# The order of the three products of a split weight piece on TensorE

## The chip, the cores and the metric

The kernel runs on one core of one Trainium2 chip. The metric is the device time of one launch, in microseconds (us): the median of the runs shown, lower is better. The profile is of one execution on the same kind of chip.

## The reference, cut to what matters

Two transformer blocks run one after the other on a sequence of 256 rows of width 2048, in float32. What matters here are the dense products: activations times weight matrices.

```python
proj = h @ w_in                                  # first block, 9,296 columns
return x + gate[:, None, :] * (concat([ya, yb]) @ w_out)
z = h @ w_in + b_in                              # second block, 8,200 columns
m = sigmoid(g_attn) * (attn @ w_attn_o) + sigmoid(g_pool) * (pool @ w_pool_o)
return m @ w_out
return (gelu(gate) * val) @ w_down               # gate, val from h @ w_up, convolved over 3 rows
```

Between them stand RMS norms, two attentions in the first block, one attention and a windowed mean in the second. The second block has 16 rows more (its meta rows), of which most products need 258 or 272 columns.

## The kernel before, in words

**Split products.** Every float32 factor is split into a rounded half (`hi`, type float32r) and the remainder (`lo`, also float32r). A product is then the sum of three matmuls: `w_lo`·`a_hi`, `w_hi`·`a_lo` and `w_hi`·`a_hi`. All add up in the same PSUM bank.

**Pieces and panels.** A weight matrix comes in pieces of 128 x 1024 floats: two blocks of 128 input rows (`kp` = 2) by 512 output columns. A panel is 512 output columns; it takes J = 8 pieces (4 where only 1024 input rows are there). Its four groups of 128 output columns go to four PSUM banks. The weights are the stationary operand and the activations (256, 258 or 272 columns) stream past. So a piece is 4 banks x 2 blocks x 3 products = 24 matmuls, and a bank collects products over all pieces of its panel. The class `Job` lists the panels in their order: qidx0, strip, qidx1, qk_a (4 panels), v_a (2), qk_b (4), v_b (2), z_a (2), z_b (2), out_a (4), out_b (4), qkv2 (6), f2, u2 (2), g2 (8), attn_o (3), pool_w, attn_o3, pool_o (4), out2 (4), up (22), down (11). The panels strip and f2 write one bank only, bank 3. The job pool_w and the job down have matmul code of their own (L1042 and after, L1100 and after), the rest go through `panel` of `pe_program` (L731).

**The path of a piece.** There are four slots for raw, `hi` and `lo` each. SyncE issues the DMA into `raw[s]` once `lo_ready[s]` tells that the old content was used. ScalarE (`split`, L1170) copies it rounded into `w_hi[s]` and raises `hi_ready[s]`; before that it waits for `used[s]`, which TensorE raises with the last matmul of the piece that had the slot. VectorE (`split`, L1660) waits for `hi_ready[s]`, subtracts, writes `w_lo[s]` and raises `lo_ready[s]`. TensorE waits for `lo_ready[s]` at the head of the piece.

**The banks.** In the last piece of a panel the last matmul of bank b raises `acc_ready[b]`. ScalarE or VectorE then takes the bank out of PSUM and raises `acc_free[b]`. In the first piece of the next panel TensorE waits for `acc_free[b]` ahead of its first matmul into bank b. All panels use the same four banks `acc`, but for `up`, where the panels alternate between `acc` and `val` (the other four, named psum_x and psum_y in the profile).

**Who takes the banks out.** This is written by hand as steps behind a certain piece of the next panel, in the queue of that engine, one bank after the other:
- ScalarE, behind the split of piece 2: `stored` (L1273) for qidx, v and z panels; with a second instruction per bank (`squares`, L1277) for qk_a and qk_b, and the bank is freed by this second one; `biased` (L1415) for qkv2, u2, g2; `mixed_stored` (L1539 and L1542) for out2, where ScalarE then also waits for its own second instruction before it goes on to the next bank; `conv_first` (L1593) for up.
- VectorE, behind the split of piece 1: `residual` for out_a and out_b, `times_gate` for attn_o and pool_o (both are recorded at L1654, the line of the helper `stt`).

In the panels of a hardware loop (`Fori`) the instructions that take out a bank have addresses that the engine computes in registers, behind its wait. At the end of out_b and of out2 the squares of the new values are summed (L955, L958), and the next panel can't begin before the norm that follows from them.

**Work between pieces.** TensorE does small matmuls and transposes of the attention behind certain pieces (`after`), in program order. Where `acts` is given, TensorE also waits at each piece for the activations' `lo` half, which VectorE makes behind its split of a piece.

Of the kernel before, what the change touches and what calls it, by code (L numbers as in the profile page):

```python
# [28 lines left out]
P = 128  # L29
# [78 lines left out]
def at_least(eng, sem, value):  # L108

    if isinstance(value, int) and value <= 0:  # L110
        return
    eng.wait_ge(sem, value)
# [10 lines left out]
def ada_sums(M, g):  # L123

    return (M.ada_first, M.ada_acc)[g // 2][:, (g % 2) * PIECE:(g % 2 + 1) * PIECE]


class Chain:
# [5 lines left out]
    def step(self, ins, wait=True):  # L134
        ins.then_inc(self.sem, 1)
        self.n += 1
        if wait:
            self.wait()
# [586 lines left out]
def pe_program(M, pe):  # L725

    job = M.job
# [3 lines left out]
    def panel(job, i, after={}, acts=None, pair=None, value=None):  # L731

        acc, ready, free = (M.acc, M.acc_ready, M.acc_free) if value is None else (M.val, M.val_ready, M.val_free)
        stored = [n + (i if pair is None else pair) for n in job.free0] if value is None else [value] * 4
        for j in range(job.J):
            s = j % SLOTS
            pe.wait_ge(M.lo_ready[s], job.raw0 + job.turn(i, j) + 1)
            if acts is not None:  # L740
                pe.wait_ge(M.act_ready, acts + job.kp * (j + 1))
            for b in job.banks:
                col = 0 if len(job.banks) == 1 else b * P
                out = acc[b][:, 0:job.N]
                if j == 0:
                    at_least(pe, free[b], stored[b])
                for k in range(job.kp):
                    c = job.kp * j + k
                    last = c == job.kp * job.J - 1
                    a_hi, a_lo = job.rhs(c)  # L750
                    w_hi = M.hi[s][:, k * job.cols + col:k * job.cols + col + P]
                    w_lo = M.lo[s][:, k * job.cols + col:k * job.cols + col + P]
                    pe.matmul(out, w_lo, a_hi, start=c == 0, stop=False)  # L753
                    pe.matmul(out, w_hi, a_lo, start=False, stop=False)  # L754
                    ins = pe.matmul(out, w_hi, a_hi, start=False, stop=last)  # L755
                if j == job.J - 1:
                    ins.then_inc(ready[b], 1)
            if j < job.J - 1:
                ins.then_inc(M.used[s], 1)
            for step in after.get(j, ()):  # L760
                step()

    def transpose(out, src, rows=P):
        return pe.transpose(out, src, ident[0:rows, 0:rows])
# [10 lines left out]
    for k in range(DC):  # L775
        out = M.acc[k % 4]
# [3 lines left out]
        for t in range(2):  # L780
            ins = transpose(out[:, META + t * P:META + (t + 1) * P], M.x_rows[:, t * D + k * P:t * D + (k + 1) * P])
# [13 lines left out]
    for g in range(4):  # L795
        pe.wait_ge(M.lo_ready[3], 4 * (g + 1))
        for m in range(8):
            ins = pe.matmul(M.X[:, 8 * g + m:8 * g + m + 1], ada_sums(M, g)[:, m * P:(m + 1) * P],
                            ones[:, 0:1], start=True, stop=True)
        ins.then_inc(M.ada_cols, 1)  # L800


    panel(job["qidx0"], 0, acts=M.mk["qidx0"])
    panel(job["strip"], 0)

    def k_idx_sums():
# [7 lines left out]
    def k_idx_twice():  # L814
# [3 lines left out]
                  ).then_inc(M.kd_ready, 1)  # L818

    panel(job["qidx1"], 0, {0: [k_idx_sums], 5: [k_idx_twice]})  # L820


# [90 lines left out]
    b = job["qk_b"]  # L913
# [128 lines left out]
    for j in range(4):  # L1042
        pe.wait_ge(M.lo_ready[j], w.raw0 + 1)
        pe.wait_ge(M.act_ready, M.mk["pool_w"] + 2 * (j + 1))
        for e in range(2):
            b_ = (2 * j + e) % 4
            pe.wait_ge(M.acc_free[b_], w.free0[b_] + j // 2)
            for k in range(2):
                a_hi, a_lo = w.rhs(2 * j + k)
                w_hi = M.hi[j][:, k * 256 + e * P:k * 256 + (e + 1) * P]  # L1050
                w_lo = M.lo[j][:, k * 256 + e * P:k * 256 + (e + 1) * P]
                out = M.acc[b_][:, 0:LIVE]
                pe.matmul(out, w_lo, a_hi, start=k == 0, stop=False)
                pe.matmul(out, w_hi, a_lo, start=False, stop=False)
                ins = pe.matmul(out, w_hi, a_hi, start=False, stop=k == 1)
# [14 lines left out]
    for k in range(DC):  # L1070
        pe.wait_ge(M.sq_done, 33 + k)
        ins = pe.matmul(M.X[:, 512:512 + LIVE], ones[:, 0:P], M.sqr[:, (k % 4) * ROWS:(k % 4) * ROWS + LIVE],
                        start=k == 0, stop=k == DC - 1)
# [1093 lines left out]
```

## Time and profile before

| what | value |
|---|---|
| median of 3 runs | 2143.71 us (2142.81 to 2145.34) |
| profiled execution: span, first to last instruction | 2141.7 us |
| median less span | 2.0 us |
| TensorE matmul busy | 2010.6 us, 94% of the span |
| VectorE busy | 1282.3 us, 60% |
| ScalarE busy | 991.1 us, 46% |
| mean granted TensorE clock | 0.968 of full |

The page gives no time of its own for the profiled execution beside its span; the median of the runs stands 2.0 us over the span. Matmuls overlap in the pipeline, so the sum of their durations is over the busy time; what counts for the rate is the distance from start to start.

### The profile page before, as it was taken

The numbers are of one execution on the slowest core, as the hardware profiler recorded it, in microseconds if no ns is written. First come the engines' busy times: TensorE is split into PE (matmuls) and PEld (weight loads), VectorE is DVE, ScalarE is ACT, GpSimd is POOL, SyncE is SP. The second block draws the span as 40 slices with busy tenths as digits, with TensorE's granted clock in tenths as the row PEclk, the third lists the DMA queues.
The fourth block names the chain that finished last, engine by engine and source line by source line (L and its number), as shares of the span: only waits on it lengthen the run. The fifth ranks groups of instructions, "written<-read, shape, count | busy, mean of one in ns | idle before, by whom it ended". The sixth has DMA issues, their size and how long they took to land.

```text
span 2141.7 us, 39022 instructions
## 1 busy us (share of the span) xinstructions
PE 2010.6 (94%) x15084; PEld 1911.8 (89%) x15084; DVE 1282.3 (60%) x1565; ACT 991.1 (46%) x1429; POOL 143.8 (7%) x151
## 2 busy tenths in 40 slices
PE   4169999999999999999999999799999999999997
PEld 2169999999999899988899999699999999988886
DVE  6777885685567633444447664666556666664555
ACT  3034555554554444444344444454444444444443
POOL 0000000000002000000004111100000000000000
PEclk8579999999999999999999999899999999999999
DMA  8868665475555555644444555255655665665553
GB/s 308 307 192 286 224 196 175 137 251 182 158 168 188 156 171 157 185 145 138 146 137 142 189 189 179 78 177 174 189 178 175 185 186 177 189 204 189 193 190 124
DMA packets 179903, 391.62 MB, mean 183 GB/s; under 512 B 11955, under 2 KB 17632, under 8 KB 177376
## 3 DMA queue, kind: packets, MB, share of 16 engines
q1 hardware_dynamic: 178800, 388.03, 57.0%
q10 hardware_dynamic: 1024, 2.51, 0.3%
q8 instruction: 54, 0.88, 0.2%
q14 instruction: 25, 0.20, 0.0%
HBM read 388.39 MB, written 2.10 MB: 182 GB/s over the span
## 4 chain that ended last, share of the span: by engine, by line
PE 89%; DVE 4%; DMA 4%; ACT 2%; issue 1%; DVEq 0%; SPq 0%; POOLq 0%; POOL 0%; ACTq 0%
PE acc L753 20%; PE acc L755 20%; PE acc L754 20%; DMA raw<-in_w_ada 4%; PE psum_y L754 2%; PE psum_y L755 2%; PE psum_x L754 2%; PE psum_x L755 2%; PE psum_y L753 2%; PE psum_x L753 2%; PE acc L1123 2%; PE acc L1122 2%; PE acc L1121 2%; PE psum_y L1123 1%; PE psum_x L1123 1%
## 5 line engine op out<-in xcount | busy, mean ns | idle before, releaser
L1660 DVE TENSOR_TENSOR w_lo<-raw,w_hi 128x1024 fp32r<-128x1024 f32 (+1 forms) x644 | 814.0, 1271 | 727.2 <-ACT w_hi L1170 723.9
L1170 ACT ACTIVATE w_hi<-raw 128x1024 fp32r<-128x1024 f32 (+1 forms) x644 | 675.2, 1050 | 929.1 <-PE acc L755 602.4
L753 PE MATMUL acc<-act_hi,w_lo 128*128 128x258 f32 (+2 forms) x3424 | 983.5, 287 | 16.9 <-issue 9.3
L755 PE MATMUL acc<-act_hi,w_hi 128*128 128x258 f32 (+2 forms) x3424 | 974.9, 285 | 0.0
L754 PE MATMUL acc<-act_lo,w_hi 128*128 128x258 f32 (+2 forms) x3424 | 972.8, 284 | 0.0
L753 PEld LDWEIGHTS acc<-act_hi,w_lo 128*128 128x128 f32 x3424 | 651.9, 190 | 27.7 <-issue 26.2
L754 PEld LDWEIGHTS acc<-act_lo,w_hi 128*128 128x128 f32 x3424 | 650.4, 190 | 0.7 <-issue 0.5
L755 PEld LDWEIGHTS acc<-act_hi,w_hi 128*128 128x128 f32 x3424 | 650.7, 190 | 0.0
L754 PE MATMUL psum_y<-act_lo,w_hi 128*128 128x258 f32 x352 | 100.1, 284 | 0.0
L755 PE MATMUL psum_y<-act_hi,w_hi 128*128 128x258 f32 x352 | 100.0, 284 | 0.0
L754 PE MATMUL psum_x<-act_lo,w_hi 128*128 128x258 f32 x352 | 99.8, 284 | 0.0
L755 PE MATMUL psum_x<-act_hi,w_hi 128*128 128x258 f32 x352 | 99.8, 283 | 0.0
L753 PE MATMUL psum_y<-act_hi,w_lo 128*128 128x258 f32 x352 | 99.4, 282 | 0.0
L753 PE MATMUL psum_x<-act_hi,w_lo 128*128 128x258 f32 x352 | 99.3, 282 | 0.0
L1123 PE MATMUL acc<-w_hi,down_hi 128*128 128x512 f32 x176 | 69.3, 394 | 0.0
L1122 PE MATMUL acc<-w_lo,down_hi 128*128 128x512 f32 x176 | 69.0, 392 | 0.0
L1121 PE MATMUL acc<-w_hi,down_lo 128*128 128x512 f32 x176 | 68.3, 388 | 0.0
L716 POOL TENSOR_TENSOR ffn_act<-gelu_gate,conv_val 128x1024 f32 x11 | 34.5, 3135 | 503.5 <-DVE conv_val L1654 503.5
L753 PEld LDWEIGHTS psum_y<-act_hi,w_lo 128*128 128x128 f32 x352 | 67.2, 191 | 0.0
L755 PEld LDWEIGHTS psum_y<-act_hi,w_hi 128*128 128x128 f32 x352 | 66.9, 190 | 0.0
L754 PEld LDWEIGHTS psum_y<-act_lo,w_hi 128*128 128x128 f32 x352 | 66.8, 190 | 0.0
L755 PEld LDWEIGHTS psum_x<-act_hi,w_hi 128*128 128x128 f32 x352 | 66.8, 190 | 0.0
(291 smaller groups left out, 2186.6 us busy)
## 6 DMA issues: line engine op xcount, KB each, us to landing
raw<-in_w_in SPq DMA_DIRECT2D x272, 512.0 KB, 3.6
raw<-in_w_ffn_up SPq DMA_DIRECT2D x176, 512.0 KB, 3.9
raw<-in_w_ffn_down SPq DMA_DIRECT2D x88, 512.0 KB, 3.5
raw<-in_w_ada SPq DMA_DIRECT2D x64, 512.0 KB, 5.2
raw<-in_w_out SPq DMA_DIRECT2D x64, 512.0 KB, 4.1
ada_x<-in_w_ada SPq DMA_DIRECT2D x16, 1024.0 KB, 7.3
raw<-in_w_attn_o SPq DMA_DIRECT2D x16, 512.0 KB, 3.6
raw<-in_w_pool_o SPq DMA_DIRECT2D x16, 512.0 KB, 4.4
```

Source lines behind the costliest of these rows:

```text
L716: pool.tensor_tensor(M.F[:, ds(i * 4 * SEQ, 4 * SEQ)], M.gg[:, :], M.vt[:, :], ALU.mult).then_inc(M.F_ready, 1)
L753: pe.matmul(out, w_lo, a_hi, start=c == 0, stop=False)
L754: pe.matmul(out, w_hi, a_lo, start=False, stop=False)
L755: ins = pe.matmul(out, w_hi, a_hi, start=False, stop=last)
L1121: pe.matmul(out, d_lo, w_hi, start=start, stop=False)
L1122: pe.matmul(out, d_hi, w_lo, start=False, stop=False)
L1123: ins = pe.matmul(out, d_hi, w_hi, start=False, stop=stop)
L1170: act.activation(M.hi[s][:, 0:job.width], M.raw[s][:, 0:job.width], ACT.Copy).then_inc(M.hi_ready[s], 1)
L1660: dve.tensor_tensor(M.lo[s][:, 0:job.width], M.raw[s][:, 0:job.width], M.hi[s][:, 0:job.width].bitcast(FP32), ALU.subtract).then_inc(M.lo_ ...
```

## The change

TensorE waits at the head of a piece for the rounded half only. For all banks and blocks it runs `w_hi`·`a_lo` and `w_hi`·`a_hi` (16 matmuls). Then it waits for the remainder half and runs `w_lo`·`a_hi` for all banks and blocks (8 matmuls). The signals `acc_ready[b]` and `used[s]` are raised by the last matmul as before, which is now one of the last eight. No other engine's code is changed.

```diff
         for j in range(job.J):
             s = j % SLOTS
-            pe.wait_ge(M.lo_ready[s], job.raw0 + job.turn(i, j) + 1)
+            pe.wait_ge(M.hi_ready[s], job.hi0 + job.turn(i, j) + 1)
             if acts is not None:
                 pe.wait_ge(M.act_ready, acts + job.kp * (j + 1))
             for b in job.banks:
@@
                 for k in range(job.kp):
                     c = job.kp * j + k
-                    last = c == job.kp * job.J - 1
                     a_hi, a_lo = job.rhs(c)
                     w_hi = M.hi[s][:, k * job.cols + col:k * job.cols + col + P]
+                    pe.matmul(out, w_hi, a_lo, start=c == 0, stop=False)
+                    pe.matmul(out, w_hi, a_hi, start=False, stop=False)
+            pe.wait_ge(M.lo_ready[s], job.raw0 + job.turn(i, j) + 1)
+            for b in job.banks:
+                col = 0 if len(job.banks) == 1 else b * P
+                for k in range(job.kp):
+                    c = job.kp * j + k
+                    a_hi, a_lo = job.rhs(c)
                     w_lo = M.lo[s][:, k * job.cols + col:k * job.cols + col + P]
-                    pe.matmul(out, w_lo, a_hi, start=c == 0, stop=False)
-                    pe.matmul(out, w_hi, a_lo, start=False, stop=False)
-                    ins = pe.matmul(out, w_hi, a_hi, start=False, stop=last)
+                    ins = pe.matmul(acc[b][:, 0:job.N], w_lo, a_hi, start=False, stop=c == job.kp * job.J - 1)
                 if j == job.J - 1:
                     ins.then_inc(ready[b], 1)
             if j < job.J - 1:
```

## Rows read from the trace of the kernel before

**Rows 1.** The page: busy us, share of the span, instructions of each engine.
```profile
PE 2010.6 (94%) x15084; PEld 1911.8 (89%) x15084; DVE 1282.3 (60%) x1565; ACT 991.1 (46%) x1429; POOL 143.8 (7%) x151
```

**Rows 2.** The page: the chain that ended last, by engine.
```profile
PE 89%; DVE 4%; DMA 4%; ACT 2%; issue 1%; DVEq 0%; SPq 0%; POOLq 0%; POOL 0%; ACTq 0%
```

**Rows 3.** The page, groups: busy us, mean ns | idle us before, releaser.
```profile
L753 PE MATMUL acc<-act_hi,w_lo 128*128 128x258 f32 (+2 forms) x3424 | 983.5, 287 | 16.9 <-issue 9.3
```

**Rows 4.** Waits of TensorE: waiter <- releaser: total us, times, longest.
```profile
PE acc L753 <- DVE act_lo L1654: 5.7, 5, 3.8
PE acc L753 <- ACT store L1273: 1.2, 2, 0.6
```

**Rows 5.** Timeline of VectorE in qidx0: start us, us, instruction [idle <-releaser].
```profile
139.19 1.23 DVE L1660 TENSOR_TENSOR w_lo<-raw,w_hi 128x1024 fp32r<-128x1024 f32 x1 [0.46 <-ACT w_hi L1170]
141.39 0.88 DVE L1654 SCALAR_TENSOR_TENSOR act_lo<-squares,shift,act_hi 128x256 fp32r<-128x256 f32 x2 [0.18 <-ACT act_hi L1199]
```

**Rows 6.** Windows: length, PE, PEld, DVE, ACT, POOL busy (instructions), clock, DMA share, GB/s.
```profile
612.00:655.00 43.00, 43.00 (x382) 43.00 (x380) 29.67 (x45) 21.58 (x28) 0.33 (x1) 1.00 0.53 173
655.00:701.00 46.00, 46.00 (x392) 46.00 (x391) 30.52 (x33) 21.82 (x28) 14.11 (x12) 1.00 0.64 199
735.00:855.00 120.00, 120.00 (x955) 120.00 (x955) 47.43 (x40) 51.15 (x59) 0.00 (x0) 1.00 0.58 171
1250.00:1343.00 93.00, 93.00 (x771) 93.00 (x771) 43.92 (x42) 46.23 (x69) 12.70 (x16) 1.00 0.56 184
708.70:712.70 4.00, 4.00 (x18) 4.00 (x19) 3.24 (x8) 1.69 (x4) 0.00 (x0) 0.50 0.00 0
```

**Rows 7.** Timeline, end of the first v_a panel.
```profile
315.90 0.28 PE L755 MATMUL acc<-act_hi,w_hi 128*128 128x256 f32 x1
316.22 0.39 ACT L1273 ACTIVATE store<-acc 128x256 f32<-128x256 f32 x1 [0.34 <-PE acc L755]
```

**Rows 8.** Timeline, end of the second g2 panel, in a loop.
```profile
971.33 0.28 PE L755 MATMUL acc<-act_hi,w_hi 128*128 128x258 f32 x1
971.78 0.48 ACT L1415 ACTIVATE gates<-acc,bias_gates 128x258 f32 x1 [0.25 <-PE acc L755]
```

**Rows 9.** Timeline, from the last qkv2 panel to f2.
```profile
855.62 0.29 PE L755 MATMUL acc<-act_hi,w_hi 128*128 128x272 f32 x1
855.94 0.58 ACT L1415 ACTIVATE qkv<-acc,bias_qkv,scale_qkv 128x272 f32<-128x272 f32 x1 [0.18 <-PE acc L755]
856.67 0.36 PE L753 MATMUL acc<-act_hi,w_lo 128*128 128x272 f32 x1 [0.76 <-ACT qkv L1415]
```

**Rows 10.** Groups by shape: instructions that take out banks; busy us, mean ns.
```profile
L1654 DVE SCALAR_TENSOR_TENSOR gates<-gates,acc 128x258 f32<-128x258 f32 x24 | 10.1, 423 | 10.5 <-PE acc L755 10.4
L1654 DVE SCALAR_TENSOR_TENSOR rT<-acc,gate,rT 128x256 f32<-128x256 f32 x20 | 9.3, 481 | 4.0 <-PE acc L755 4.0
```

**Rows 11.** Timeline of ScalarE at the end of a qk_a panel.
```profile
236.78 0.37 ACT L1273 ACTIVATE store<-acc 128x256 f32 x1
237.04 0.38 ACT L1277 ACTIVATE squares<-acc 128x256 f32<-128x256 f32 x1
237.31 0.39 ACT L1273 ACTIVATE store<-acc 128x256 f32 x1
```

**Rows 12.** Timeline of ScalarE at the end of the first out2 panel.
```profile
1272.54 0.48 ACT L1539 ACTIVATE gates<-acc,cols 128x258 f32 x1 [0.24 <-ACT squares L1542]
1272.91 0.38 ACT L1542 ACTIVATE squares<-acc 128x258 f32<-128x258 f32 x1
1273.53 0.48 ACT L1539 ACTIVATE gates<-acc,cols 128x258 f32 x1 [0.24 <-ACT squares L1542]
```

**Rows 13.** Timeline, end of the last out2 panel.
```profile
1342.80 0.29 PE L755 MATMUL acc<-act_hi,w_hi 128*128 128x258 f32 x1
1342.94 0.48 ACT L1539 ACTIVATE gates<-acc,cols 128x258 f32<-128x258 f32 x1
1343.81 0.48 ACT L1539 ACTIVATE gates<-acc,cols 128x258 f32<-128x258 f32 x1
```

## The prediction

> **What bounds the kernel now.** I read the page's busy shares first, then the chain, the groups, the waits of TensorE, and last the timeline around each place where one panel follows another. TensorE is busy 94% of the span [rows 1] and makes up 89% of the chain that ended last [rows 2]; no other engine has more than 4%. The reader is to see in the groups how little is left to win: before the first product of a bank and block (L753, the one that the old order puts behind the wait for the remainder) TensorE was idle 16.9 us in all its 3424 executions on `acc` [rows 3]. In the waits the idle time that is put down to an engine's work ends with `act_lo` (5.7 us, 5 times) or with ScalarE taking out a bank (1.2 us, 2 times) [rows 4]; the rest, 9.3 us put to issue [rows 3], stands behind the norms ahead of qkv2 and up. None ends with `w_lo`. So the weights' remainder is nowhere late, and the program is a stream of matmuls whose length is count times distance. That distance is m = 0.1126 us in out_a (382 in 43.00 us), 0.1173 in out_b, 0.1257 in qkv2 (272 columns), 0.1206 in out2 (258 columns) [rows 6].
>
> **Part 1, the earlier start: 0 us.** The head of a piece waits for `w_hi` instead of `w_lo`, some 1.2 us sooner [rows 5]. In the stream both have been there for long. Where TensorE does wait with weights at stake, in qidx0, it waits for `act_lo`, and VectorE writes that behind the `w_lo` of the same piece: `w_lo` starts at 139.19, the two `act_lo` end at 142.27 [rows 5]. The new order still needs `act_lo` in its first matmul, so nothing starts sooner. Bounds: a loss is excluded, since `w_hi` is always there before `w_lo`; a gain is at most the 5.7 us of rows 4. I take 0. The second wait, now in the middle of a piece, is met; what queues behind it is the rest of TensorE's own stream, and everyone waits for that. Nothing is issued anew: the same 24 matmuls and weight loads per piece, no DMA moved, and `used[s]` is raised at the same place of the stream, so ScalarE's splits and SyncE's transfers keep their times.
>
> **Part 2, the distance of the matmuls: 0 us.** The same pairs come as before (each load of `w_hi` twice, `w_lo` once; `a_hi` streams twice, `a_lo` once). Only the neighbours change, and a bank changes every 4 and every 2 matmuls instead of every 6. The trace doesn't show that order. The nearest rows are those of out_a and out_b, 4.7 ns apart for the same 256 columns [rows 6]; they differ in where the activations lie, which the change leaves alone, so I take a tenth of it, 0.5 ns, to either side: 13,152 matmuls in `panel` (548 piece-equivalents of 24) times 0.5 ns = 6.6 us either way.
>
> **Part 3, the banks are ready later: +18 us.** This is what the change costs. The last matmul of bank b in a panel used to stand 6(3-b) matmuls ahead of the panel's last one, now 2(3-b). Bank 0 was ready 18 matmuls before the end, 2.1 us; now 6, 0.7 us. And the next panel reaches bank b after 4b matmuls, not 6b. Call the start of the last matmul 0. Then:
> - The engine starts taking out a bank d after the start of its last matmul: 316.22 - 315.90 = 0.32 us [rows 7]; in a hardware loop 971.78 - 971.33 = 0.45 us, because the addresses are computed behind the wait [rows 8].
> - TensorE starts r after the bank was taken out: 856.67 - (855.94 + 0.58) = 0.15 us [rows 9]. For VectorE I take the same r and d.
> - Bank 0 is free for TensorE at -6m + d + e + r, with e the time it takes; TensorE would come at m. Stall: d + e + r - 7m. Banks 1 to 3 add (p - 4m) each where the period p from bank to bank is over 4m, about 0.48.
>
> By kind of boundary (e from rows; where waits are met, instructions of ScalarE follow each other 0.1 us before the end of the last, as 0.37 us ones every 0.27 [rows 11]):
> - qk_a, qk_b, 8 boundaries, copy and squares: e = 0.27 + 0.38 = 0.65, p = 0.53 [rows 11], m = 0.118 (out_b's, rounded up). Loop: 0.45 + 0.65 + 0.15 - 0.83 = 0.42, and 3 x 0.06 = 0.18: 0.6 us, 6 times; outside a loop 0.47, twice. Together 4.5 us.
> - out2, 3 boundaries in a loop: e = 0.37 + 0.38 = 0.75 and p = 1273.53 - 1272.54 = 0.99, because ScalarE waits for its own result [rows 12]. 0.45 + 0.75 + 0.15 - 0.84 = 0.51, and 3 x (0.99 - 0.48) = 1.53: 2.04 us, together 6.1 us.
> - The end of out2, whose sums TensorE and the norm wait for: the period is 0.87 there, the last copy starts at 1343.81 [rows 13]. New: bank 0 is ready at 1342.80 - 0.72 + 0.32 = 1342.40, the last copy starts 3 x 0.87 later, at 1345.01: +1.2 us on the path. At the end of out_b VectorE is still at a split when bank 0 gets ready, nothing changes.
> - qkv2, 5 in a loop: e = 0.58 [rows 9]: 0.45 + 0.58 + 0.15 - 0.88 = 0.30, together 1.5 us. From qkv2 to f2, which needs bank 3 at once: four in a row with p = 0.47 from -0.43 on end at 1.56, TensorE starts at 1.71 instead of 856.67 - 855.62 = 1.05 [rows 9]: 0.65 us. The same from qidx0 to strip with short copies: 0.1.
> - g2: e = 0.48 [rows 8]. Loop 0.24, 6 times; outside 0.11, twice: 1.7 us.
> - out_a and out_b on VectorE: e = 0.48 [rows 10]. 0.32 + 0.48 + 0.15 - 0.79 = 0.16, 4 times; in out_b's loop 0.45 + 0.48 + 0.15 - 0.82 = 0.26, 3 times: 1.4 us.
> - attn_o and pool_o: e = 0.42 [rows 10]: 0.05, 6 times, and 0.18 in a loop, twice: 0.7 us.
> - u2 0.08 twice; 8 boundaries with one copy of 0.39 us [rows 7]: 0.02 each; up to down, where VectorE's two steps per bank follow: 0.3. Together 0.6 us.
> - up, 22 panels: 0. They alternate between two sets of banks, a set has a whole panel of time.
>
> Sum: 4.5 + 6.1 + 1.2 + 1.5 + 0.65 + 0.1 + 1.7 + 1.4 + 0.7 + 0.6 = 18.4 us. What hid the taking out of the banks before were the 2.1 us of other banks' matmuls; with 0.7 us the cover is gone. A stall of TensorE adds in full, as nothing else limits the stream behind it. Bounds of this part: 12 us, if only the squares, out2 and half of the rest come as worked out; 24 us, if in loops the waits keep ScalarE from overlapping (p = e + 0.05: 0.14 x 3 x 5 = 2 us more in qkv2, 0.05 x 3 x 6 = 1 us in g2, 0.2 x 6 in qk) and d is 0.1 longer than read at a dozen places.
>
> Against span: 2141.7 + 18.4 = 2160.1; the median of the runs lies 2.0 us above the span, which gives 2162.1 us, 0.86% slower.
>
> What the rows show on cover (bank 0 taken out beside 18 matmuls into other banks) is also a rule of the Trainium skill, Perfetto Trace Analysis, Optimizing Tensor Performance, Matmuls: "Independent matmul groups should rotate through different PSUM banks so the ACT/DVE evacuation of one overlaps the next group's matmuls". By it this change goes the wrong way, since it closes all four groups nearly together; the size it leaves to the trace. The same page, Matmul Optimizations, wants all 8 banks used, which here only `up` does, where I count no loss.
>
> **The rivals.**
> 1. *The matmuls come closer together, and the kernel is faster.* The place is the distance within the stream. For it: the same 256 columns are seen at 112.6 and 117.3 ns [rows 6], so something beside the columns counts, and it may be which weights load beside which stream. Against: every pair of load and stream of the new order exists in the old one. It decides from 18.4 us / 13,152 = 1.4 ns on; at 3 ns it gives 2162 - 39 = 2123 us. 4%.
> 2. *The earlier start counts.* If TensorE's waits in qidx0 were in truth for the weights, 5.7 us return and the boundaries still cost: 2156 us. Against it speaks rows 4. 4%.
> 3. *The banks are taken out in time.* If r and d are shorter where TensorE isn't idle yet, short copies cost nothing and only out2 is left, its end included: 7 us, 2151 us; with out2's period pressed too, 2145 us. For it: d is read against modelled ends of matmuls. Against: the wait from qkv2 to f2 shows d and r end to end. 10%, of which 3 points within 0.2% of before.
> 4. *Stalls pull the clock down.* Behind the idle time ahead of qkv2, one of the two that make up the 9.3 us of rows 3, the granted clock is 0.50, the 1.2 GHz level, and 4 us hold 18 matmuls (0.222 us each, not 0.126) [rows 6]. Some 20 matmuls at that level cost 2 us; at the 11 boundaries of qk and out2 that is 22 us: 2184 us. Against: behind 0.76 us of idle at f2 [rows 9] the next matmuls are at full rate, and my stalls are 0.5 us pieces. 6%.
>
> **How the numbers follow.** Forecast 76%, with 2151 to 2173 as its own range (12 to 24 us, and the 6.6 us of the distance taken partly). I predict 2162 us. The range 2150 to 2174 leaves out rival 1, rival 4 and the lowest part of rival 3. A measurement tells about 0.2% (4.3 us) from no change. Faster: 4%, from rival 1. Same: 5%, from rival 3 and a weak form of 1. Slower: 91%.
>
> **What would show it.** Right: at the head of out2 panels TensorE idles about 0.5 us four times, ended by ScalarE's L1542; at qk panels by L1277; at qkv2 and g2 by L1415, once each; none in up. The waits of TensorE for ScalarE and VectorE at banks grow from some 2 us (1.2 in rows 4, 0.76 in rows 9) to some 19 us; the count of matmuls per us within the windows away from boundaries stays within 0.5%. Wrong: if the window counts change by over 1%, part 2 fails; if boundaries of qkv2 and g2 show no idle time, d or r fails; if idle time ends with `w_lo`, part 1 fails.

## The result, and the profile after

The changed kernel takes 2161.65 us (median of 4 runs, 2160.96 to 2163.53) against 2143.26 us (4 runs, 2141.08 to 2145.34): a ratio of 1.0087 with a 95% interval of 1.0073 to 1.0101. It is 18.4 us slower; 2162 us had been forecast. The profiled execution has a span of 2159.4 us, 1.9 us under its time, and a granted clock of 0.97 as before.

The page of the changed kernel: busy us, share and instructions of each engine; the chain by engine; the three products in `panel`, which are now L751, L752 and L760 (busy us, mean ns | idle us before, releaser).

```profile
PE 2023.0 (94%) x15084; PEld 1914.0 (89%) x15084; DVE 1277.7 (59%) x1565; ACT 977.7 (45%) x1429; POOL 150.5 (7%) x151
PE 88%; DVE 4%; DMA 4%; ACT 2%; issue 2%; ACTq 0%; DVEq 0%; SPq 0%; POOLq 0%; POOL 0%
L751 PE MATMUL acc<-act_lo,w_hi 128*128 128x258 f32 (+2 forms) x3424 | 865.4, 289 | 23.5 <-issue 9.3
L752 PE MATMUL acc<-act_hi,w_hi 128*128 128x258 f32 (+2 forms) x3424 | 849.8, 284 | 0.0
L760 PE MATMUL acc<-act_hi,w_lo 128*128 128x258 f32 (+2 forms) x3424 | 485.9, 284 | 0.0
```

The counts of instructions on these engines are the same [rows 1]. Only the first product of a bank waits, as before, and its idle time went from 16.9 [rows 3] to 23.5 us. The product with the remainder, L760, waits for nothing: its own wait in the middle of a piece costs nothing. The busy time of TensorE rose by 12.4 us with the same matmuls. That isn't work, for the matmuls are the same: a matmul that is held at the head of a bank is recorded longer, and its neighbours cover part of the stall, as the timeline below shows.

The waits of TensorE in the changed kernel (waiter <- releaser: total us, times, longest):

```profile
PE acc L751 <- issue: 9.3, 2, 4.7
PE acc L751 <- DVE act_lo L1659: 6.1, 6, 3.8
PE acc L751 <- ACT squares L1547: 3.2, 12, 0.3
PE acc L751 <- ACT qkv L1420: 1.4, 1, 1.4
PE acc L751 <- ACT store L1278: 1.3, 2, 0.7
PE acc L751 <- ACT squares L1282: 1.0, 6, 0.2
```

New against [rows 4] are 12 waits for the second instruction of out2 and 6 for that of the qk panels; the one wait for `qkv` is that of f2, 0.76 us before [rows 9]; the 5.7 us for `act_lo` are still there, 6.1 now, and `w_lo` is still in no row.

The timeline of TensorE in the changed kernel at the first boundary between two out2 panels, and its waits at the next two of that panel's banks (start us, us, instruction [idle <-releaser]):

```profile
1309.09 0.76 PE L760 MATMUL acc<-act_hi,w_lo 128*128 128x258 f32 x5
1310.17 0.39 PE L751 MATMUL acc<-act_lo,w_hi 128*128 128x258 f32 x1 [0.31 <-ACT squares L1547]
1310.39 0.28 PE L752 MATMUL acc<-act_hi,w_hi 128*128 128x258 f32 x1
...
1311.16 0.39 PE L751 MATMUL acc<-act_lo,w_hi 128*128 128x258 f32 x1 [0.25 <-ACT squares L1547]
1312.16 0.39 PE L751 MATMUL acc<-act_lo,w_hi 128*128 128x258 f32 x1 [0.25 <-ACT squares L1547]
```

ScalarE there:

```profile
1309.37 0.48 ACT L1544 ACTIVATE gates<-acc,cols 128x258 f32 x1 [1.26 <-PE acc L760]
1309.74 0.38 ACT L1547 ACTIVATE squares<-acc 128x258 f32<-128x258 f32 x1
1310.36 0.48 ACT L1544 ACTIVATE gates<-acc,cols 128x258 f32 x1 [0.24 <-ACT squares L1547]
```

The last of the five remainders ends at 1309.85, so it began at 1309.57. From there to 1310.17 are 0.60 us where 0.12 is the distance: a stall of 0.48 us, of which the idle column shows 0.31. ScalarE takes a bank every 0.99 us, and TensorE then follows at 1311.16 and 1312.16, at that same period. The matmul behind a stalled one comes 0.22 us later instead of 0.12.

The place of the cost is seen best by cutting the trace at the first matmul of each stage. Us from one to the next in the profiled execution: the kernel before, and what each kernel has on top of it. (The last four are experiments 1 to 4 below.)

```
stretch                     before   changed last_old ends_old last_new out2_later
qidx0 to qk_a                 58.70     0.14    -0.05     0.05     0.26     0.16
qk_a (4 panels)              104.58     2.13    -0.22    -0.18     1.87     2.15
v_a                           47.30     0.22    -0.16    -0.18     0.35     0.16
qk_b (4)                     114.04     2.12    -0.21    -0.13     1.65     2.13
v_b                           47.35     0.16    -0.18    -0.16     0.26     0.12
z_a to out_a                 112.05     0.09    -0.14     0.06     0.45    -1.41
out_a to qkv2 (8)             96.42     2.36    -0.02     0.01     2.98     3.18
qkv2 to f2 (6)               148.00     2.81    -0.62    -0.26     2.10     2.07
f2 to g2                      54.93     0.01    -0.23    -0.17     0.15     0.01
g2 to attn_o (8)             239.47     1.37    -0.51    -0.35     1.47     1.35
attn_o to out2 (8)            99.01     1.37    -0.22    -0.05     1.43     1.45
out2, first to last matmul    92.73     6.50     2.23     0.22     4.33     3.33
out2's last matmul to up      26.79    -0.69    -1.84     0.38    -0.69    -1.38
up, first to last matmul     516.33     0.84    -1.39     0.49    -0.76     0.61
up's last matmul to the end  255.78     0.14    -0.01    -0.02     0.16     0.13
sum                         2013.47    19.59    -3.58    -0.31    16.00    14.06
```

Together 19.6 us. The start of qidx0 lies at 128.23 before and 126.39 in the changed kernel, which makes the difference of the spans 17.8 us; that start varied from 125.28 to 128.64 among the eleven kernels profiled here.

### The profile page after: what moved, and what is told of

It is laid out like the page before. It is cut to its first block, busy times and chain, and to the rows that moved or that the text cites. A ratio compares the mean times of both kernels' runs of the same rounds, so it can differ in the third digit from the quotient of the medians.

```text
span 2159.4 us, 39115 instructions
## 1 busy us (share of the span) xinstructions
PE 2023.0 (94%) x15084; PEld 1914.0 (89%) x15084; DVE 1277.7 (59%) x1565; ACT 977.7 (45%) x1429; POOL 150.5 (7%) x151
## 3 DMA queue, kind: packets, MB, share of 16 engines
q10 hardware_dynamic: 1024, 2.51, 0.3%
## 4 chain that ended last, share of the span: by engine, by line
PE 88%; DVE 4%; DMA 4%; ACT 2%; issue 2%; ACTq 0%; DVEq 0%; SPq 0%; POOLq 0%; POOL 0%
PE acc L751 21%; PE acc L752 20%; PE acc L760 19%; DMA raw<-in_w_ada 4%; PE psum_x L760 2%; PE psum_y L751 2%; PE psum_y L752 2%; PE psum_x L752 2%; PE psum_y L760 2%; PE psum_x L751 2%; PE acc L1128 2%; PE acc L1127 2%; PE acc L1126 2%; PE psum_x L1128 1%; PE psum_y L1128 1%
## 5 line engine op out<-in xcount | busy, mean ns | idle before, releaser
L751 PE MATMUL acc<-act_lo,w_hi 128*128 128x258 f32 (+2 forms) x3424 | 865.4, 289 | 23.5 <-issue 9.3
L752 PE MATMUL acc<-act_hi,w_hi 128*128 128x258 f32 (+2 forms) x3424 | 849.8, 284 | 0.0
L751 PEld LDWEIGHTS acc<-act_lo,w_hi 128*128 128x128 f32 x3424 | 651.4, 190 | 43.1 <-issue 28.3
L752 PEld LDWEIGHTS acc<-act_hi,w_hi 128*128 128x128 f32 x3424 | 653.1, 191 | 0.7 <-issue 0.5
L760 PE MATMUL acc<-act_hi,w_lo 128*128 128x258 f32 (+2 forms) x3424 | 485.9, 284 | 0.0
L760 PEld LDWEIGHTS acc<-act_hi,w_lo 128*128 128x128 f32 x3424 | 444.1, 190 | 0.0
L752 PE MATMUL psum_y<-act_hi,w_hi 128*128 128x258 f32 x352 | 89.1, 284 | 0.0
L751 PE MATMUL psum_y<-act_lo,w_hi 128*128 128x258 f32 x352 | 89.1, 285 | 0.0
L752 PE MATMUL psum_x<-act_hi,w_hi 128*128 128x258 f32 x352 | 88.3, 283 | 0.0
L751 PE MATMUL psum_x<-act_lo,w_hi 128*128 128x258 f32 x352 | 88.2, 282 | 0.0
L752 PEld LDWEIGHTS psum_y<-act_hi,w_hi 128*128 128x128 f32 x352 | 67.4, 192 | 0.0
L751 PEld LDWEIGHTS psum_y<-act_lo,w_hi 128*128 128x128 f32 x352 | 67.2, 191 | 0.0
L751 PEld LDWEIGHTS psum_x<-act_lo,w_hi 128*128 128x128 f32 x352 | 66.9, 190 | 0.0
L752 PEld LDWEIGHTS psum_x<-act_hi,w_hi 128*128 128x128 f32 x352 | 66.9, 190 | 0.0
L760 PE MATMUL psum_x<-act_hi,w_lo 128*128 128x258 f32 x352 | 57.6, 286 | 0.0
L760 PE MATMUL psum_y<-act_hi,w_lo 128*128 128x258 f32 x352 | 56.5, 283 | 0.0
```

Of the source, the lines that this page charges most:

```text
L751: pe.matmul(out, w_hi, a_lo, start=c == 0, stop=False)
L752: pe.matmul(out, w_hi, a_hi, start=False, stop=False)
L760: ins = pe.matmul(acc[b][:, 0:job.N], w_lo, a_hi, start=False, stop=c == job.kp * job.J - 1)
```

## The experiments

The kernels of experiments 1 to 4 ran beside the same 21 runs of the kernel before (2143.18 us). The ratios are to the kernel before.

**1. `last_old`: the old order in the last piece of a panel alone.** It shows what the banks' late closing costs, and leaves the earlier start and the new order in all other pieces.

```diff
+            if j == job.J - 1:
+                ...   # wait for lo_ready at the head; per bank w_lo*a_hi, w_hi*a_lo, w_hi*a_hi
+            else:
+                ...   # the changed order
```

> The changed kernel, but in the last piece of each panel the three products of a bank stand together as before, behind the wait for the remainder; all other pieces keep the new order. Theory A (banks are ready late and are needed early): the banks of a panel are ready 18, 12, 6 and 0 matmuls before its end again, so the stall on bank 0 goes everywhere. What stays is that the first piece of the next panel comes to bank b after 4b matmuls, not 6b. By the times of the kernel before that matters in out2 alone: bank 3 is free at 2.02 + 0.15 us after the panel's start and is wanted at 1.45, some 0.7 us with the restart, and bank 2 some 0.2: 2.7 us over three boundaries. 2146 us. TensorE waits on L1282 and L1420 at no boundary of qk, qkv2 or g2. Rival B (the order within a piece costs time by itself, 1.4 ns per matmul): 7 of 8 pieces keep the new order, 2143.3 + 16 = 2159 us.

2143.16 us (11 runs; before 2143.18, 21 runs), ratio 0.9996 (0.9987 to 1.0005). B is refuted: with the banks closed early the loss is gone. A said 2146: its 2.7 us in out2 came as 2.23, but in the trace the other stretches from qidx0 on became shorter, up by 1.4 us and the rest by 0.0 to 0.6 each, together 4.0 us, and the one from out2 to up by 1.8 more (on that one see part 3 below). The trace is of the fastest of the 11 executions (2136.97 us), so its span says less than the median. The waits:

```profile
PE acc L769 <- ACT squares L1565: 0.7, 3, 0.3
PE acc L769 <- DVE act_lo L1677: 5.6, 5, 3.8
```

3 waits at banks of out2 instead of 12 and none for the qk panels; the wait for `act_lo` stays. From start to start there are two stalls per boundary, at bank 2 (0.30 us where 0.12 is the distance) and at bank 3 (0.53).

**2. `ends_old`: the old order in the first and the last piece,** the new one in between.

```diff
+            if j in (0, job.J - 1):
+                ...   # the old order, the wait for lo_ready at the head
```

> The changed kernel with the old order in the first and the last piece of each panel; the 6 (of 8) or 2 (of 4) pieces between keep the new one. Theory A: nothing is left of the cost, and the earlier start is worth nothing: 2143.3 us, within 0.1% of before. Rival B (order costs by itself): 0.7 of the pieces are new, 2143.3 + 13 = 2156 us. Rival C (the earlier start does bring something that the boundaries hid): faster than before, by up to the 5.7 us of TensorE's waits for act_lo, 2138 us.

2143.09 us (11 runs), ratio 0.9998 (0.9989 to 1.0008). A is confirmed; B (2156) and C's 2138 are refuted, and a gain of more than 2.4 us lies outside the interval. In most of the program's pieces the new order costs nothing and brings nothing that could be measured, neither by the earlier start nor by the distance (out_a to qkv2 0.01, up 0.49 over 516 us).

**3. `last_new`: the kernel before with the new order in the last piece alone.**

```diff
+            if j < job.J - 1:
+                ...   # the old order
+            else:
+                ...   # the changed order
```

> The kernel before with the new order in the last piece of each panel alone. Theory A: the stalls on bank 0 are those of the changed kernel, since they come from when the bank is ready. Banks 1 to 3 are wanted every 6 matmuls again (0.71 us), so the qk panels lose their second part (0.3 us at 8 boundaries, 2 us less with the restarts counted) and out2 half of it (0.8 us at 3 boundaries). 18.4 - 1.2 to 2 - 2.4 = 14 to 15 us over before: 2158 us. Rival B (the order costs by itself): one piece in eight is new, 2143.3 + 2.5 = 2146 us.

2158.11 us (5 runs), ratio 1.0067 (1.0053 to 1.0081): A (2158) is confirmed, B (2146) refuted. One piece of four or eight carries 14.9 of the 18.4 us. Its waits are the changed kernel's, but for out2:

```profile
PE acc L754 <- ACT squares L1300: 1.0, 6, 0.2
PE acc L754 <- ACT squares L1565: 0.9, 3, 0.3
PE acc L754 <- ACT qkv L1438: 1.4, 1, 1.4
```

In out2 the row counts one wait a boundary and not four. The stalls at banks 1 to 3 are still there from start to start, 0.29 to 0.30 us where 0.12 is the distance, but the changed kernel has 0.53 to 0.54: in the old first piece TensorE takes 0.72 us per bank, ScalarE 0.99. The stretch costs 4.33 us, not 6.50. That the new first piece reaches the banks sooner is thus worth 2.2 us in out2 and 0.7 in the two qk stretches. Of the 3.6 us by which the two traces differ, another 1.6 lie in up, where no bank is waited for.

**4. `out2_later`: the changed kernel, and ScalarE waits for its own squares one bank later in out2.**

```diff
-                act.wait_ge(M.acc_free[m], o2.free0[m] + i + 1)
-                act.sem_inc(M.sq_done, 1)
+                if m > 0:
+                    act.wait_ge(M.acc_free[m - 1], o2.free0[m - 1] + i + 1)
+                    act.sem_inc(M.sq_done, 1)
+            act.wait_ge(M.acc_free[3], o2.free0[3] + i + 1)
+            act.sem_inc(M.sq_done, 1)
```

> The changed kernel, with one thing more: in out2 ScalarE waits for the end of a bank's squares only behind the next bank's two instructions (behind the last bank at once), so it no longer idles 0.24 us per bank. Theory A: the period from bank to bank falls from 0.99 to some 0.65 to 0.7 us (0.37 from copy to squares, 0.28 to the next copy); the stall on banks 1 to 3 is period less four matmuls, so each loses 0.3 us: 2.8 us at the three boundaries, and 0.7 us at the end of out2: 2161.7 - 3.5 = 2158 us. The stall on bank 0 stays, 0.5 us. Rival D (the period is set by the durations 0.48 + 0.38 of the two instructions, not by the wait): period 0.86, 1 us less, 2160.5 us. Rival E (the stalls at out2 come from TensorE's own restart): no change, 2161.7 us.

2158.47 us (5 runs), ratio 1.0067 (1.0053 to 1.0081), 3.2 us under the changed kernel, whose runs weren't taken beside these and whose interval overlaps. So the time alone leaves rival D open (2160.5 us, a period of 0.86); the trace decides. ScalarE at the same boundary as above:

```profile
1308.56 0.48 ACT L1544 ACTIVATE gates<-acc,cols 128x258 f32 x1 [1.26 <-PE acc L760]
1309.19 0.48 ACT L1544 ACTIVATE gates<-acc,cols 128x258 f32 x1
1309.82 0.50 ACT L1544 ACTIVATE gates<-acc,cols 128x258 f32 x1
```

The period is 0.63 instead of 0.99, and TensorE's row of waits there goes from 12 times to 3 (from start to start 0.17 to 0.18 us are left at banks 1 to 3, where it was 0.53):

```profile
PE acc L751 <- ACT squares L1547: 0.9, 3, 0.3
```

The stretch of out2 costs 3.33 us instead of 6.50: half of the largest item was ScalarE's wait for itself, which the kernel before hid behind the other banks' matmuls.

**5 to 7. The distance of the matmuls.** The prediction's rival 1 rested on 112.6 against 117.3 ns for 256 columns [rows 6]. The stages with the larger distance read activations that lie 272 floats apart in one buffer, out_a reads another buffer where they lie 256 apart. `before_close` takes the old order and lays the first block's activations 256 floats apart; `before_off16` also moves them by 64 bytes, `before_off176` by 704 bytes, which is where out_a's buffer starts against the weights' (832 against 128, modulo 1024).

```diff
-        return M.act_hi[:, ROWS * k + c0:ROWS * k + c0 + n], M.act_lo[:, ROWS * k + c0:ROWS * k + c0 + n]
+        at = (SEQ * k if n == SEQ else ROWS * k) + c0           # before_close
+        at = (SEQ * k + 16 if n == SEQ else ROWS * k) + c0      # before_off16
+        at = (SEQ * k + 176 if n == SEQ else ROWS * k) + c0     # before_off176
+        return M.act_hi[:, at:at + n], M.act_lo[:, at:at + n]
```

(Each kernel has one of the three lines; the helpers that write these activations change alike and are left out here.)

> The kernel before (old order), with the activations of the first block 256 floats apart instead of 272 (all panels with 256 columns but out_a, whose activations lie 256 apart already). The prediction said that out_a and out_b are 4.7 ns per matmul apart because of where the activations lie; the changed kernel's first out_a panel, at out_b's distance with its activations unmoved, casts doubt on it. Theory L (the layout sets the distance): 3936 matmuls come 4.4 ns closer, 17 us: 2126 us. Theory P (it is something of the stream's history, not of the layout): 2143 us, distance 0.118 in the windows of v_a and out_b.

2146.71 us (11 runs; before 2143.17, 15 runs), ratio 1.0015 (1.0006 to 1.0024). Both theories missed: the panels ran at an even 120.0 ns where the kernel before, in v_a, alternates between 119.7 and 117.7 from piece to piece.

> The kernel before with the first block's activations 256 floats apart and begun 16 floats (64 bytes) into their buffer. In before_close all of these panels came at an even 0.120 us per matmul, in out_a at 0.1133. Weight buffers and these activations begin at the same byte within 1024 (128), out_a's activations at 832. Theory L1 (what counts is the distance of the two starts modulo 128 bytes: 0 gives 0.120, 64 gives 0.1133): 3936 matmuls come 5 ns closer than in the kernel before, 20 us: 2123.5 us. Theory L2 (a coarser distance counts, 192 or 704 bytes as in out_a): no more than 2 us of change, or 0.120 again, 2143 to 2147 us.

2140.10 us (10 runs; before 2143.64, 13 runs), ratio 0.9981 (0.9972 to 0.9991), mostly 117.8 ns. L1 (2123.5) is refuted; the time lies between it and L2's.

> As before_off16, but begun 176 floats (704 bytes) into the buffer, so that the activations stand to the weights exactly as out_a's do, modulo 1024 bytes. Theory L1 and L2 both: 0.1133 us per matmul in the 20.5 panel-equivalents of the first block, 20 us less than before: 2123.5 us. Theory P (the distance in out_a is not from the layout): 0.120 as in before_close, 2147 us.

2132.31 us (4 runs, 2127.38 to 2136.09; before the same 13 runs), ratio 0.9942 (0.9925 to 0.9958). The forecast of L1 and L2 was 2123.5, that of P 2147: both missed. In the trace, which is of the slowest of the four executions, 73 of the 164 pieces concerned stood at 113.3 ns (nearly all of v_a, most of qk_a) and 54 at 117.8 (all of out_b). The same window in v_a of four kernels (length, then busy us and instructions of PE, PEld, DVE, ACT, POOL, clock, DMA share, GB/s): before,

```profile
316.00:338.00 22.00, 22.00 (x188) 22.00 (x187) 15.65 (x29) 9.42 (x11) 0.00 (x0) 1.00 0.69 206
```

`before_close`,

```profile
316.00:338.00 22.00, 22.00 (x186) 22.00 (x185) 16.04 (x31) 8.76 (x12) 0.00 (x0) 1.00 0.68 208
```

`before_off16`,

```profile
316.00:338.00 22.00, 22.00 (x189) 22.00 (x189) 14.53 (x29) 9.80 (x12) 0.61 (x1) 1.00 0.69 201
```

and `before_off176`, with its window of out_a:

```profile
316.00:338.00 22.00, 22.00 (x192) 21.90 (x192) 14.54 (x25) 9.73 (x12) 2.00 (x2) 1.00 0.72 215
612.00:655.00 43.00, 43.00 (x368) 43.00 (x367) 31.15 (x47) 18.37 (x23) 0.33 (x1) 1.00 0.56 186
```

The count in 22 us goes 186, 188, 189, 192 with TensorE busy in all of them. The surprise is the last row: out_a, whose own buffer, weights and order weren't touched, has 368 matmuls in 43 us where it had 382 [rows 6]. Where the operands start matters, but it doesn't decide alone. The likely reading is that what ran ahead of a stage has a part in it; that wasn't tested by itself. `before_off176` is 11 us under the kernel before and 29 under the changed one.

**8. `wide16`: off176 and the second block's activations 288 floats apart, moved by 64 bytes.** (Two small buffers make room; that part of the edit is left out.)

```diff
-    M.act_hi = put("act_hi", [P, DC * ROWS], F32R)
+    M.act_hi = put("act_hi", [P, DC * 288], F32R)
...
+        at = (SEQ * k + 176 if n == SEQ else 288 * k + 16) + c0
```

> before_off176, and in the second block the activations 288 floats (1152 bytes, 9 x 128) apart instead of 272, begun 16 floats (64 bytes) in; two small buffers of the first attention moved to make room. Theory L1 (the start of the stream against that of the weights modulo 128 bytes sets the distance: 0.120 at 0, 0.1133 or 0.1177 at 64): all 258-column panels but g2 and attn_o stand at 64 now and should come closer than their 0.1208, by 2 to 6 ns over 5,376 matmuls of pool_o, out2 and up, and the 272-column ones (1,632) too: 2132 - 14 to - 40, say 2108 us. Theory L2 (only distances that are equal modulo 1024 help): some 2132 us, with 0.1208 in up.

2131.26 us (5 runs; before 2144.23, 9 runs), ratio 0.9947 (0.9929 to 0.9964). Within its interval it is `before_off176`: against the kernel before, up gained 2.29 us and qkv2 0.64, g2 lost 1.43. L2 was right in the time (2132), and nearly in the distance: up stood at 120.1 ns instead of 120.8. The large gain of L1 isn't to be had this way.

**9. `after_off176`: the changed kernel with the layout of `before_off176`.**

> The changed kernel (new order) with the layout of before_off176. Theory A: the boundaries cost what they cost in the changed kernel, a little more where the matmuls are closer (7m is 0.79 instead of 0.83 us): 18.4 + 1 over before_off176's 2132.3: 2151.5 us. Theory Q (part of the 18 us was a distance that the layout also sets): less than 12 us over it, under 2144 us.

2152.15 us (5 runs), ratio 1.0044 (1.0029 to 1.0058) to the kernel before, 19.8 us over `before_off176` (2132.31), which ran beside other runs. A (2151.5) is confirmed, Q (under 2144) refuted. With another layout, and with matmuls some 5% closer in part of the panels, the new order costs about the same, as a price paid at boundaries should.

## Why the prediction was right

**Part 1, the earlier start, 0 us: right.** No idle time ends with `w_lo`, before or after. The waits for `act_lo` stayed (5.7 and 6.1 us), and `ends_old`, which keeps the earlier start in the middle pieces, gains nothing that its interval shows (-2.4 to +1.7 us).

**Part 2, the distance, 0 us: right in size, with a reason that was too simple.** The windows in up, before and then changed:

```profile
1600.00:1700.00 100.00, 100.00 (x830) 100.00 (x829) 60.53 (x67) 47.28 (x55) 6.27 (x2) 1.00 0.61 181
```

```profile
1600.00:1700.00 100.00, 100.00 (x829) 100.00 (x828) 62.55 (x74) 46.66 (x57) 6.28 (x2) 1.00 0.59 178
```

830 and 829 matmuls in 100 us. Over all 22 panels of up it is 0.84 us, 0.2 ns a matmul. But the prediction put the difference of the two distances of rows 6 down to where the activations lie, which the change leaves alone. In the changed kernel the first panel of out_a ran at 117.8 instead of 113.3 ns (0.48 us longer, restart included), and v_a went from 119.7 and 117.7 by turns to 118.5 and 118.0; `last_old` is 4.0 us shorter than before in its stretches other than out2 and the one behind it. So the distance does answer to the order a little, to either side. By the prediction's own sign (a count that changes by over 1% away from boundaries) part 2 failed in that one panel of out_a, by 4%; in v_a (188 and 187 matmuls in 22 us) and in up it held. The bound of 6.6 us held too; the reason given for it, the layout alone, didn't.

**Part 3, the banks, 18.4 us: right in mechanism and in most of its terms; that the sum came out to a tenth is in part luck.** Measured in the table, with the forecast in brackets: qk_a and qk_b 4.3, 4.6 with what falls into the head of v_a and v_b (4.5); out2 6.5 (6.1); qkv2 and f2 2.8 (2.15); out_a and out_b 2.4 (1.4); g2 1.4 (1.7); attn_o and pool_o 1.4 (0.7); up 0.8 (0; no gap at its boundaries is over 0.13 us, so this is no wait at a bank). In the traces the stretches add up to 19.6 us, and that with 1.1 us net that the clock gave back: 1.9 us behind out2, less 0.75 at the head of qkv2 (both below). Without the clock it would be 20.7 us. The pieces that the terms were made of:
- d, from the last matmul of bank 0 to ScalarE: that matmul started 6 x 0.12 before 1309.57, at 1308.85, ScalarE at 1309.37: 0.52 us in a loop (0.45). In the loops of qk and g2 it was 0.44 and 0.45, in that of qkv2 0.53; VectorE took 0.54 to 0.56 in out_b's loop and 0.39 at attn_o, where 0.45 and 0.32 had been taken. r, from the bank taken out (1309.74 + 0.38) to TensorE: 0.05 (0.15). At out2 d and r were each off by up to a tenth of a us and their sum, 0.57 against 0.60, by less: the two errors cancel.
- The stall at the head of out2 is 0.48 us (0.51), and the other three banks cost 1.65 (1.53): 2.12 us a boundary against 2.04. At a qk boundary 0.33 in the gap and 0.33 in the first piece (0.42 and 0.18).
- Not in the sum was the start after a stall: the second matmul comes 0.19 to 0.23 us after the first, up to 0.1 us more than in the stream, and it does so even where the stall itself is only 0.02 to 0.06 us (0.14 to 0.18 us from start to start at v_a, attn_o and out_a). It makes most of what attn_o and pool_o (in pool_o 0.14 us in the first piece, beside gaps up to 0.12 over the distance), out_a and out_b cost over their terms.
- qkv2 to f2: the timelines of TensorE and of ScalarE,

```profile
862.28 1.18 PE L760 MATMUL acc<-act_hi,w_lo 128*128 128x272 f32 x8
864.87 0.36 PE L751 MATMUL acc<-act_lo,w_hi 128*128 128x272 f32 x1 [1.41 <-ACT qkv L1420]
```

```profile
862.74 1.99 ACT L1420 ACTIVATE qkv<-acc,bias_qkv,scale_qkv 128x272 f32<-128x272 f32 x4 [1.58 <-PE acc L760]
```

The last remainder started at 862.28 + 1.18 - 0.29 = 863.17, f2 1.70 us later: 0.65 us more than the 1.05 of [rows 9], as worked out. Some 0.75 us more in qkv2 isn't the banks': its first panel ran 26 matmuls 0.23 us apart, at a granted clock of 0.50, where it had been 19.
- The end of out2: the last copy started 2.20 us behind the last matmul (at 1362.46, the matmul at 1360.26), where it had been 1.01 [rows 13]. That is the 1.2 us of the forecast. Yet the stretch up to `up` became 0.69 us shorter. The next windows show why: the last 24 of the matmuls between out2 and up that sum squares, before and then changed.

```profile
1357.60:1365.00 7.40, 7.37 (x24) 5.82 (x24) 1.89 (x2) 4.24 (x11) 0.00 (x0) 0.74 0.00 0
```

```profile
1376.20:1381.80 5.60, 5.49 (x24) 4.48 (x24) 1.95 (x2) 4.22 (x12) 0.00 (x0) 1.00 0.00 0
```

The same 24 took 7.37 us at a granted clock of 0.74 and 5.49 at 1.00, the 2.4 GHz level throughout. What the banks cost, the clock gave back. This may well belong to the change: of the eleven kernels profiled, the five with the new order in the first or the last piece of a panel (or in both) all took 5.49 us at 1.00 for these 24, and the six with the old order in both, `ends_old` among them, 7.33 to 7.79 us at 0.70 to 0.74. How the order would do it isn't shown, and no term of the prediction covers it.

**Rivals 2 and 3 fell**, rival 2 with experiment 2, rival 3 with the trace: the banks are not taken out in time, and short copies cost too (g2, attn_o, pool_o). **Rival 4 fell**: the granted clock is 1.00 over out2's boundaries (1310.39 to 1340.00 and 1315 to 1355) and in up, and the matmuls behind a stall are at 0.12 us but for the first. **Rival 1** was right that something beside the columns counts and wrong that this change would bring the matmuls closer by much: it moved the distance a little, to either side.

**One sign was badly put.** "Waits for banks grow from some 2 us to some 19" isn't what the view shows: they grow from 2.0 to 6.9 us in it, and g2, attn_o, out_a and the qkv2 loop have no row of their own of any size. Read in that view, the sign "no idle time at qkv2 and g2: d or r fails" would have spoken against a part that was right. A matmul is recorded 0.28 us long where the next starts 0.12 us after it, so the first 0.16 us of each stall is hidden in the record of the last matmul, and a part in the longer record of the next. By the start-to-start distance the stalls are there, 0.15 us a boundary in g2, 0.28 to 0.30 in qkv2. What the view leaves out of these and of the longer stalls, and the restarts, is the rest.

**The rule of the Trainium skill held.** The banks closed nearly together cost 18.4 us, and in up, whose panels alternate between two sets of banks, the first matmul of a panel comes at most 0.123 us after the last one before it, as in the stream. That is what the Trainium skill asks for (Perfetto Trace Analysis, Optimizing Tensor Performance, Matmuls: rotate the groups through banks so that taking out one overlaps the next one's matmuls); the trace agrees, by the two numbers.

What stays open: what sets the two or three distances of the matmuls, what the 0.1 us at a restart are, and why the clock behind out2 was at 0.74 in the one kernel and at 1.00 in the other.

## What to carry to other kernels

Where several banks close in one piece, finish each bank with all its products before the next: the time until the banks are ready is the cover for taking them out, and the cost of giving it up can be worked out per boundary as d + e + r less the matmuls in between (here with up to 0.1 us for the restart), before anything is built. An earlier start is worth only what a wait row puts down to the thing waited for. Read stalls of TensorE from start to start, not from the idle column, when its records overlap.

## What the runs showed of the hardware that was not expected

- The distance of two matmuls of 256 float32r columns, each with its weight load, took values near 113.3, 117.8 and 120.0 ns, with the same instructions. It changed with the start of the streamed activations against the weights: equal modulo 128 bytes (128 and 128, 256 floats apart) 120.0; moved by 64 bytes 117.8; moved by 704 bytes 113.3 in 73 pieces and 117.8 in 54 of 164. Over the program that is 14 us from `before_close` to `before_off176`. A stage that isn't touched (out_a) can go from 113.3 to 117.8 when the one ahead of it changes. Three offsets were tried, so this is an observation and no rule.
- After a stall at a bank, however short, TensorE's second matmul came 0.19 to 0.23 us behind the first instead of 0.12 (out2 0.22, attn_o 0.22 behind a stall of 0.03 to 0.04).
- In a hardware loop ScalarE started 0.44 to 0.55 us behind the start of the bank's last matmul (qk 0.44, g2 0.45, qkv2 0.53 to 0.55, out2 0.52 to 0.54), outside one 0.32 to 0.33 (862.41 to 862.74 at f2).
- The granted clock behind out2 went with the order of the products: 1.00 in the five kernels with the new order in the first or last piece, 0.70 to 0.74 in the six with the old one there, over the same 24 matmuls. Not explained.
